# Gated delta rule on one core: the second tile's solve with the key-state product taken before the inverse

## The reference, cut to what matters

```python
lhs = A + jnp.eye(C, dtype=f32)
rhs = jnp.concatenate([vc * bc[..., None], kb * jnp.exp(gc)[..., None]], axis=-1)
sol = lax.linalg.triangular_solve(lhs, rhs, left_side=True, lower=True, unit_diagonal=True)
u_hat, w = sol[..., :dv], sol[..., dv:]
...
    u = u_hat_i - jnp.einsum('bhcd,bhdv->bhcv', w_i, state)
    o = jnp.einsum('bhcd,bhdv->bhcv', q_dec_i, state) + jnp.einsum('bhcm,bhmv->bhcv', attn_i, u)
    state = state * gl_i[..., None, None] + jnp.einsum('bhcd,bhcv->bhdv', k_dec_i, u)
```

## Time and profile before

| | before |
|---|---|
| median of the runs (three) | 812.03 us |
| the profiled execution | 812.03 us |
| its span, first to last instruction | 810.7 us |
| mean granted TensorE clock, share of full | 0.998 |
| PE busy | 801.4 us, 99% |
| DVE busy | 592.6 us, 73% |
| ACT busy | 449.3 us, 55% |
| POOL busy | 79.3 us, 10% |

### The profile page before, as it was taken

One profiled execution on the slowest core, in us unless ns is written; L12 is line 12 of the kernel. 1 busy time (PEld: TensorE's weight loads), 2 busy tenths in 40 slices (PEclk: granted clock), 3 DMA queues, 4 the chain that ended last, 5 costly groups with the idle time before them and its releaser, 6 DMA issues.

```text
span 810.7 us, 13987 instructions
## 1 busy us (share of the span) xinstructions
PE 801.4 (99%) x5622; PEld 724.0 (89%) x5622; DVE 592.6 (73%) x979; ACT 449.3 (55%) x733; POOL 79.3 (10%) x67
## 2 busy tenths in 40 slices
PE   7999999999999999999999999999999999999998
PEld 5999998999999988899999998888778888888886
DVE  6888979875545676769999997486866877778543
ACT  5666567554445455546565664366665655565441
POOL 0001000011011502101111110011100111011000
PEclk9999999999999999999999999999999999999999
DMA  7755564647324455574788666464425656555541
GB/s 262 235 157 157 167 233 143 173 130 217 119 66 133 147 171 194 176 239 158 232 214 255 216 213 207 156 208 155 157 78 151 205 190 208 181 184 202 191 158 71
DMA packets 126096, 144.14 MB, mean 178 GB/s; under 512 B 11456, under 2 KB 102736, under 8 KB 125776
## 3 DMA queue, kind: packets, MB, share of 16 engines
q1 hardware_dynamic: 123584, 141.19, 54.7%
q10 hardware_dynamic: 2448, 2.05, 1.0%
HBM read 141.78 MB, written 1.46 MB: 177 GB/s over the span
## 4 chain that ended last, share of the span: by engine, by line
PE 97%; DVE 1%; DMA 1%; ACT 0%; issue 0%; POOL 0%; ACTq 0%; DVEq 0%; POOLq 0%
PE bank L577 95%; PE bank L624 1%; DMA h<-in_x 1%; PE bank L921 0%; PE bank L646 0%; PE bank L870 0%; DVE fox_p L1762 0%; PE bank L894 0%; PE bank L701 0%; DVE panel_lo L1517 0%; PE bank L803 0%; ACT fox_p L1205 0%; ACT panel_hi L1053 0%; DVE x_halves L1538 0%; ACT x_halves L1053 0%
## 5 line engine op out<-in xcount | busy, mean ns | idle before, releaser
L1517 DVE TENSOR_TENSOR panel_lo<-panel_raw,panel_hi 128x1024 fp32r<-128x1024 f32 x252 | 315.0, 1253 | 147.9 <-ACT panel_hi L1053 147.0
L577 PE MATMUL bank<-x_halves,panel_hi 128*128 128x256 f32 (+1 forms) x1952 | 417.3, 305 | 1.5 <-DVE x_halves L1538 1.5
L1053 ACT ACTIVATE panel_hi<-panel_raw 128x1024 fp32r<-128x1024 f32 x252 | 266.2, 1059 | 163.7 <-PE bank L577 161.6
L577 PEld LDWEIGHTS bank<-x_halves,panel_hi 128*128 128x128 f32 x1952 | 317.0, 192 | 17.2 <-issue 1.7
L577 PE MATMUL bank<-x_halves,panel_lo 128*128 128x256 f32 x1152 | 325.6, 283 | 0.0
L577 PEld LDWEIGHTS bank<-x_halves,panel_lo 128*128 128x128 f32 x1152 | 220.5, 191 | 0.0
L577 PE MATMUL bank<-panel_hi,x_halves 128*128 128x512 f32 x256 | 80.6, 396 | 0.0
L577 PE MATMUL bank<-panel_hi,act_hi 128*128 128x512 f32 x176 | 68.6, 390 | 0.0
L577 PE MATMUL bank<-panel_hi,act_lo 128*128 128x512 f32 x176 | 68.5, 389 | 0.0
L577 PE MATMUL bank<-panel_lo,act_hi 128*128 128x512 f32 x176 | 68.5, 389 | 0.0
L577 PEld LDWEIGHTS bank<-panel_hi,x_halves 128*128 128x128 f32 x256 | 46.7, 188 | 9.9 <-DVE panel_lo L1517 0.6
(11 more groups left out here) (284 smaller groups left out, 936.0 us busy)
## 6 DMA issues: line engine op xcount, KB each, us to landing
panel_raw<-in_w_in SPq DMA_DIRECT2D x38, 1024.0 KB, 5.2
panel_raw<-in_w_up SPq DMA_DIRECT2D x30, 1024.0 KB, 5.4
panel_raw<-in_w_down SPq DMA_DIRECT2D x20, 1024.0 KB, 5.0
panel_raw<-in_w_gate SPq DMA_DIRECT2D x10, 1024.0 KB, 5.3
panel_raw<-in_w_out SPq DMA_DIRECT2D x8, 1024.0 KB, 5.0
panel_raw<-in_w_in SPq DMA_DIRECT2D x12, 512.0 KB, 4.6
panel_raw<-in_w_branch_fox SPq DMA_DIRECT2D x4, 1024.0 KB, 5.0
panel_raw<-in_w_branch_gdn SPq DMA_DIRECT2D x4, 1024.0 KB, 5.0
```

Of the source, the lines that this page charges most:

```text
L577: return e.matmul(o, l, r, start=start, stop=stop, skip_group_check=True)
L1053: return e.activation(o, i_, ACT.Copy, scale=scale)
L1517: e.tensor_tensor(lo, raw_view(i, k0, kt), hi.bitcast(F32), ALU.subtract).then_inc(s_lo, 1)
```

## The change

The second tile's solve is written the other way round. `solve_known` (step 62) multiplies the second tile's keys by `S1` into a bank `known`; DVE adds them, scaled by minus the decay, to the values in place (`tok_v`); `solve_second` (step 63) multiplies the result once by the inverse. `nw`, `nwT` and `tok_kbe` go. The keys are kept for it by ACT at steps 39 and 40 in `kT_second`, since `XT` overwrites `kT`; the decay gets its minus at step 29. `solve_out` moves to step 64, the squares to 65, their sums to 66, means, power and gate product to 67. Both halves of `o0` are copied by ACT.

```diff
@@ -824,10 +823,8 @@
                 for c, (kind, _) in enumerate(CONVS):
                     if kind == "v":
                         e.wait_ge(*emptied(("conv_turn", c)))
-                e.wait_ge(s_kbe, HEADS)
                 for b in range(2):
                     four("u0", b, lambda q_: [(XT[:, 2 * q_, :], tok_v[:, 2 * q_, :])])
-                    four("nw", b, lambda q_: [(tok_kbe[:, q_, :], XT[:, 2 * q_ + 1, :])])
 
             def solve_state():
                 both("u0")
...
@@ -835,18 +832,23 @@
                 for b in range(2):
                     four("s1", b, lambda q_: [(tok_kdec[:, q_, :], U0[:, q_, :])])
 
-            def solve_second():
+
+            def solve_known():
                 both("s1")
-                both("nw")
-                e.wait_ge(s_qdec, 1)
+                e.wait_ge(s_k_2nd, 2)
                 for b in range(2):
-                    four("u1", b, lambda q_: [(XT[:, 2 * q_ + 1, :], tok_v[:, 2 * q_ + 1, :]),
-                                              (nwT[:, q_, :], S1[:, q_, :])])
+                    four("known", b, lambda q_: [(kT_second[:, q_, :], S1[:, q_, :])])
                 for b in range(2):
                     four("o0", b, lambda q_: [(attnT[:, 2 * q_, :], U0[:, q_, :])])
 
+            def solve_second():
+                for b in range(2):
+                    e.wait_ge(*emptied(("known", b)))
+                    four("u1", b, lambda q_: [(XT[:, 2 * q_ + 1, :], tok_v[:, 2 * q_ + 1, :])])
+
             def solve_out():
                 both("u1")
+                e.wait_ge(s_qdec, 1)
                 for b in range(2):
                     four("o1", b, lambda q_: [(qT[:, 2 * q_ + 1, :], S1[:, q_, :]), (attnT[:, 2 * q_ + 1, :], U1[:, q_, :])])
 
...
@@ -1008,8 +1010,10 @@
                 if n == 61:
                     solve_state()
                 if n == 62:
+                    solve_known()
+                if n == 63:
                     solve_second()
-                if n == 63:
+                if n == 64:
                     solve_out()
                 if n == 76:
                     e.wait_ge(s_on, 2)
...
@@ -1353,6 +1357,8 @@
                     e.wait_ge(s_gv, GV_KDEC)
                     e.activation(kdec_s, kdec_s, ACT.Exp).then_inc(s_ga, 1)
                     e.activation(egc_u, gc_u, ACT.Exp).then_inc(s_ga, 1)
+                    e.wait_ge(s_ga, GA_MINUS_EGC - 1)
+                    copy(egc_u, egc_u, -1.0).then_inc(s_ga, 1)
                 if n - 6 in CONV_AT and CONVS[CONV_AT[n - 6]][0] == "k":
                     unit_squares(CONV_AT[n - 6])
                 if n - 5 in CONV_AT:
...
@@ -1375,9 +1381,10 @@
                     e.wait_ge(s_ksq_dve, len(SQUARED_K))
                     zero(BT).then_inc(s_bt_zero, 1)
                 if n in (39, 40):
-                    heads = range(4 * (n - 39), 4 * (n - 39) + 4)
-                    scaled_keys(tok_kdec, 0, [kdec_s[:, hh:hh + 1] for hh in range(HEADS)], heads, s_kdec)
-                    scaled_keys(tok_kbe, 1, [egc_u[:, 2 * hh + 1:2 * hh + 2] for hh in range(HEADS)], heads, s_kbe)
+                    heads = slice(4 * (n - 39), 4 * (n - 39) + 4)
+                    scaled_keys(tok_kdec, 0, [kdec_s[:, hh:hh + 1] for hh in range(HEADS)], range(HEADS)[heads], s_kdec)
+                    e.wait_ge(s_gated, len(CONVS))
+                    copy(kT_second[:, heads, :], tile_of(kT, 1)[:, heads, :]).then_inc(s_k_2nd, 1)
                 if n == 41:
                     e.wait_ge(s_dec_sub, 4)
                     e.activation(tile_of(gc_row, 1), tile_of(gc_row, 1), ACT.Exp).then_inc(s_gc_exp, 1)
...
@@ -1404,17 +1412,17 @@
                         copy(X[0:64, units_8(b), :], bank_of(("x_turn2", b))[0:64].rearrange(
                             "p (u w) -> p u w", u=8)).then_inc(empties(("x_turn2", b)), 1)
                 if n == 60:
-                    four("nw", 0, nwT[:, 0:4, :], -1.0)
                     four_scaled("u0", U0, 0)
-                    four("nw", 1, nwT[:, 4:8, :], -1.0)
                 if n == 61:
                     four("s1", 1, S1[:, 4:8, :])
                 if n == 62:
+                    for b in range(2):
+                        four("o0", b, tile_of(o_tok, 0)[:, 4 * b:4 * b + 4, :])
+                if n == 63:
                     four_scaled("u1", U1, 1)
-                    four("o0", 1, tile_of(o_tok, 0)[:, 4:8, :])
-                if n == 63:
+                if n == 64:
                     four("o1", 1, tile_of(o_tok, 1)[:, 4:8, :])
-                if n == 64:
+                if n == 65:
                     for name in ("o0", "o1"):
                         for b in range(2):
                             e.wait_ge(*emptied((name, b)))
...
@@ -2056,15 +2064,23 @@
                 if n == 61:
                     four("s1", 0, S1[:, 0:4, :])
                 if n == 62:
+                    e.wait_ge(s_ga, GA_MINUS_EGC)
+                    for b in range(2):
+                        e.wait_ge(*filled(("known", b)))
+                        for hh in range(4 * b, 4 * b + 4):
+                            u = 2 * hh + 1
+                            i_ = e.scalar_tensor_tensor(tok_v[:, u, :], units(bank_of(("known", b)))[:, hh - 4 * b, :],
+                                                        egc_u[:, u:u + 1], tok_v[:, u, :], ALU.mult, ALU.add)
+                        i_.then_inc(empties(("known", b)), 1)
+                if n == 63:
                     four_scaled("u1", U1, 1)
-                    four("o0", 0, tile_of(o_tok, 0)[:, 0:4, :])
-                if n == 63:
+                if n == 64:
                     four("o1", 0, tile_of(o_tok, 1)[:, 0:4, :])
-                if n == 65:
+                if n == 66:
                     for m, s in enumerate(UNIT_HALVES):
                         e.wait_ge(s_osq, m + 1)
                         e.tensor_reduce(st[:, s], o_squares[:, s, :], AX.X, ALU.add).then_inc(s_oss, 1)
-                if n == 66:
+                if n == 67:
                     e.wait_ge(s_oss, 2)
                     e.wait_ge(s_q_eps, 1)
                     e.scalar_tensor_tensor(st[:, 0:16], st[:, 0:16], 1.0 / DH, ss_q, ALU.mult, ALU.add) \
...
```

More of the change, by code:

```diff
@@ L197 @@
 GV_ABS, GV_BETA, GV_COEF, GV_LG, GV_ROW, GV_GC, GV_KDEC = 3, 4, 5, 23, 24, 26, 27
-GA_EXP, GA_BETA, GA_COEF, GA_KDEC, GA_EGC = 1, 2, 3, 4, 5
+GA_EXP, GA_BETA, GA_COEF, GA_KDEC, GA_MINUS_EGC = 1, 2, 3, 4, 6
 def build(nc, a, out, scratch_a, scratch_x, scratch_c):
@@ L223, in build @@
         tok_v = at("tok_v", [P, UNITS, DH], 13)
-        tok_kbe = at("tok_kbe", [P, HEADS, DH], 15)
+        kT_second = at("kT_second", [P, HEADS, P], 15)
         tok_kdec = at("tok_kdec", [P, HEADS, DH], 15.5)
@@ L238, in build @@
         U1 = at("U1", [P, HEADS, DH], 20.5)
-        nwT = at("nwT", [P, HEADS, P], 12)
         S1 = at("S1", [P, HEADS, DH], 12.5)
@@ L427, in build @@
         s_qsq, s_q_eps = sem("q_squares"), sem("q_norm_eps")
-        s_qdec, s_kbe, s_kdec = sem("q_decayed"), sem("k_beta_decayed"), sem("k_decayed")
+        s_qdec, s_k_2nd, s_kdec = sem("q_decayed"), sem("second_tiles_of_kT_kept"), sem("k_decayed")
         s_dec_sub, s_dec, s_gc_exp = sem("decay_differences"), sem("decay_exp"), sem("gc_rows_exp")
```

## The result

The changed kernel took **814.64 us** (median of 5 runs, 814.53 to 815.36), the kernel before in the same session 812.03 us (5 runs, 811.12 to 812.46): slower by 2.6 us. The ratio of the two kernels is 1.0041 (95%: 1.0029 to 1.0052), where the two medians alone give 1.0032. Forecast were 813.1 us and no change, with a range up to 814.0. The profiled execution is the longest of the five, 815.36 us with a span of 814.0 us, 3.3 us more than that of before; so the traces differ by more than the medians.

A forecast was written before the change was run, and what follows sets the result against it. The prediction took PE, busy 801.4 of 810.7 us, as the bound. Products -1.79, head 6's wait +0.68 and head 7's wait +2.20 made +1.09 on 812.03, so 813.1 us (no change), range 810.0 to 814.0.

The forecast's parts named there:

- Products, -1.79: PE in the solve: 56 small products instead of 64, eight fewer, saving 1.79 us.
- The added work in steps 62 and 63, zero: DVE's eight additions (at most 2.7 us) and ACT's changed copies stay hidden behind PE's work: set at zero.
- Head 6's transpose, +0.68: Delayed squares and moved sums hold up head 6's normalisation on DVE; PE begins at 260.90, a new wait of 0.68 us.
- POOL's chain: Key bias, masks, affines, then power at about 265.05 and gate product at 267.95, just behind step 72's panel_lo at 267.70.
- Head 7's transpose, a wait of 3.6 us, +2.2: Gate product delays head 7's TENSOR_SCALARs; PE begins at 274.3, waiting 3.6 us instead of 1.41: +2.2 us.
- -1.79 + 0.68 + 2.20 = +1.09: Products, head 6's wait and head 7's wait added to 812.03 us, giving 813.1 us; chance 0.45.
- The rivals: Only products count 0.13; power before panel_lo 0.15; gate product too late 0.07; mask 0.12; change not as stated, excluded.
- The one on the slow side, the mask between head 6's TENSOR_SCALARs: A POOL mask takes the port between them; PE begins head 7's transpose at 274.85: +1.64, 813.7 us; chance 0.12.

The follow-up runs named there:

- b_shift: Kernel before with its old solve, but o1, its copies, squares, sums, means, power and gate product one step later: 816.14 us, ratio 1.0056.
- a_gz71_sums: Changed kernel with POOL's gate product behind step 70's affine and DVE's sums of step 66 behind head 6's normalisation: 808.09 us, ratio 0.9963.
- b_gz71: Kernel before with POOL's gate product moved behind step 70's affine: 809.24 us, ratio 0.9978.
- a_sums: Changed kernel with only DVE's sums of step 66 put behind head 6's normalisation, gate product left in place: 812.68 us, ratio 1.002.
- a_fill3: Changed kernel with three unread 128x512 products on PE ahead of head 7's transpose: 812.07 us, ratio 1.001.
- a_again: The changed kernel itself timed once more, in the second session of experiments: 813.1 us, ratio 1.0026.
- a_fill1: Changed kernel with one unread 128x512 product on PE ahead of head 7's transpose: 812.76 us, ratio 1.0019.

## Why the prediction was wrong

- *Products, -1.79.* Right: -1.79 in the table, 1.71 from b_shift, 1.67 from a_gz71_sums and b_gz71.
- *The added work in steps 62 and 63, zero.* Right. The eight scalar_tensor_tensor took 0.34 us each, and u1 began with no idle before it.
- *Head 6's transpose, +0.68.* Right: +0.64, released by fox_p; PE began at 260.71, forecast 260.90. a_sums showed the cause, the sums ahead of the normalisation.
- *POOL's chain.* The end was nearly right, the steps less so. The key bias landed 7.2 us after its issue (253.88 to 261.07) instead of 6.46. The power began 1.17 us after gate_f's affine, not 2, but lasted 3.87 us instead of 2.92, beside a panel_lo that ended at 264.67. If the power stood waiting until then, as forecast, its usual 2.88 us from there give 267.55; the gate product came at 267.41, forecast 267.95. It got there 0.11 us ahead of the panel_lo of step 72 instead of behind it. The prediction gave 274.3 for either order; PE began at 273.97.
- *Head 7's transpose, a wait of 3.6 us, +2.2.* Right: 3.45 us, +2.06.
- **The sum, "-1.79 + 0.68 + 2.20 = +1.09".** This is the step that failed. It priced the wait by its length. The runs showed that a wait of this length has a second price, paid after it ends: the clock falls to 1.2 GHz and step 71 takes 5.79 us instead of 3.23, +2.56, more than the wait had grown. With that term the sum is +3.65, and the trace has +3.50. a_fill3, which keeps the clock up and leaves the release where it is, has +0.86, so the rest of the sum stood. The row that could have warned me was one I used: the clock held behind 1.41 us of idle. It says nothing about 3.6 us, and I neither asked that question nor widened the range for it. The same trace had a nearer row that the prediction does not use: at 12 us the clock stands at 0.50 behind idle times of 2.07 and 1.53 us, with the mean clock of 0.998 as the sign that such a place exists.
- *The rivals.* None of the five came about. The one on the slow side, the mask between head 6's TENSOR_SCALARs, did not happen: they took 0.55 us, and the mask began at 261.07, a microsecond after the first. Its 813.7 us was nearer only by the size of its number. Its sum is also not closed: the distance of 6.63 runs from the start of the gate product, and the text adds it to the arrival of panel_lo (268.2); from its own 267.95 it would give 274.6.

What stays open is what decides whether the clock's fall costs 1.5 or 2.6 us (the wait was equal, 3.45 and 3.47, in the two executions of the changed kernel), and whether a wait of 2.5 us brings it down each time.

## What to carry to other kernels

Where one engine is busy 99% of the time, price a new wait on it by its length and then look at what the engine does after it: on TensorE a wait of 2.5 to 3.5 us here cost another 1.5 to 2.6 us at half the clock, while 1.4 us and less cost nothing more. Look also for a second idle time close by: 2.07 and 1.53 us with 1.09 us of work between them brought the clock down in the kernel before. So a chain that is moved a step later may cost more than the work that the change saves; take it apart, put the one long instruction that holds the shared port (here the gate product) where no one on the critical engine is waiting for its neighbour, and only then judge the rest of the change. And when two edits come in one change, run each alone: the solve was worth 1.1 to 1.7 us all the time, under a shift that cost 5.2.

## What the runs showed of the hardware

- TensorE's granted clock fell to 0.50 behind idle times of 2.51, 3.07, 3.45, 3.46 and 3.47 us, and stayed at 1.00 behind 0.79 and 1.41 us. It came back some 3 to 6 us after PE resumed (by the one-microsecond windows). In one of the traces (a_again) it fell only after PE had resumed.
- At the program's start every trace has two idle times with 1.09 us of work between them, the second 1.52 or 1.53 us long. Behind a first one of 2.07 (before) or 2.35 us (a_fill1) the clock fell to 0.50 for about 3.5 us; in the eight traces with a first one of 0.73 to 1.88 us it stayed at 1.00.
- The power of 16 columns on POOL took 2.92 us where DVE's panel_lo began after it, and 3.86 to 3.88 where it began inside a running panel_lo; that panel_lo took 1.55 or 1.56. This fits a power that waited for DVE to finish, while a panel_lo that began inside a running power took 1.22 to 1.23 (before, b_gz71, a_sums, a_gz71_sums). The Trainium skill, "SBUF — State Buffer", section "SBUF: two separate sides", has the port held by the first comer for its whole instruction. The trace agrees for the gate product (3.37 us for a panel_lo behind it) and does not for a panel_lo inside the power.
